# A three-block model on one core: how ten norms get their sums of squares, and how their tiles reach the products

## The reference

```python
def rms_norm(x, g):
    y = x * rsqrt(mean(x * x, axis=-1) + 1e-6)
    return y * g
# first block
h = x + stick_breaking_attention(rms_norm(x, norm_mix))
h = h + swiglu(rms_norm(h, norm_ffn))
h = h + sigmoid(rms_norm(h, norm_ple) @ w_gate) * (p @ w_proj)
x = rms_norm(h, final_norm)
# second block: gated convolution (31 taps) beside retention (4 heads)
u = rms_norm(x, norm_g) * (1 + scale) + shift
a = silu(layernorm(conv(a * sigmoid(b)))) @ conv_pw * silu(g)
h = x + gate * (concat(a, retention(u)) @ w_out)
x = rms_norm(h, final_g)
# third block: S5 beside SSD
h = x + concat(s5(rms_norm(x, norm_w)), ssd(...)) @ w_out
h = h + sigmoid(rms_norm(h, ple_norm_w) @ w_gate) * (p_3 @ w_proj)
return rms_norm(h, final_norm_w)
```

## Time and profile before

| what | value |
|---|---|
| median of 3 runs | 5034.85 us (5033.29 to 5037.63) |
| the profiled execution, its own time | 5034.92 us |
| its span | 5033.1 us |
| mean granted TensorE clock | 0.865 |
| TensorE matmuls, busy | 78% of the span |
| VectorE, busy | 51% |
| GpSimd, busy | 31% |
| ScalarE, busy | 17% |

### The profile page before, as it was taken

The page is one execution under the profiler, slowest core; times in us unless marked ns, Lnnn a source line. Parts: engine busy times, 40 slices in busy tenths (PEclk is TensorE's granted clock), DMA queues, the critical chain, the costliest instruction groups (busy, mean ns, idle before and its releaser), DMA issues.

```text
span 5033.1 us, 47576 instructions
## 1 busy us (share of the span) xinstructions
PE 3921.5 (78%) x18610; PEld 3141.9 (62%) x18610; DVE 2563.6 (51%) x2452; ACT 880.6 (17%) x1440; POOL 1549.5 (31%) x581
## 2 busy tenths in 40 slices
PE   4999996999999864777789886584996875559856
PEld 3667764878778753555556754463785764447745
DVE  5554565232332356777832342647149955444555
ACT  2433442000000022000010001202120111121021
POOL 2122213444444431555522321131323420004322
PEclk8999997989898887888899998797998976669978
DMA  1000000111111100111211111111631241112111
GB/s 65 25 26 26 22 22 30 51 51 55 49 50 50 58 29 17 59 58 58 75 46 42 56 44 58 34 58 67 121 78 55 87 131 25 25 42 75 59 34 50
DMA packets 140587, 259.59 MB, mean 52 GB/s; under 512 B 45744, under 2 KB 87728, under 8 KB 139184
## 3 DMA queue, kind: packets, MB, share of 16 engines
q1 hardware_dynamic: 50832, 156.26, 10.8%
q10 hardware_dynamic: 89632, 101.63, 6.3%
HBM read 209.35 MB, written 46.14 MB: 51 GB/s over the span
## 4 chain that ended last, share of the span: by engine, by line
PE 44%; issue 22%; DVE 18%; POOL 10%; ACT 2%; DMA 2%; ACTq 0%; POOLq 0%; DVEq 0%; SPq 0%
PE bank L474 12%; PE bank L475 11%; PE bank L476 11%; POOL wh L449 7%; POOL wl L451 3%; DVE acc L1429 2%; DVE sq L1445 1%; PE bank L685 1%; PE bank L648 1%; DVE rinv L1434 1%; DVE spill L1932 1%; DVE xl L1455 1%; PE bank L895 1%; DVE fb L1578 1%; PE bank L668 1%
## 5 line engine op out<-in xcount | busy, mean ns | idle before, releaser
L449 POOL TENSOR_TENSOR wh<-raw,mats 128x1024 fp32r<-128x1024 f32 x288 | 796.9, 2767 | 3399.4 <-PE bank L476 3347.8
L474 PE MATMUL bank<-xh,wh 128*128 128x512 f32 x3008 | 1206.8, 401 | 411.2 <-DVE xl L1455 155.9
L475 PE MATMUL bank<-xl,wh 128*128 128x512 f32 x3008 | 1194.3, 397 | 0.0
L476 PE MATMUL bank<-xh,wl 128*128 128x512 f32 x3008 | 1192.0, 396 | 0.0
L474 PEld LDWEIGHTS bank<-xh,wh 128*128 128x128 f32 x3008 | 580.9, 193 | 556.9 <-issue 295.7
L451 POOL TENSOR_TENSOR wl<-raw,wh 128x1024 fp32r<-128x1024 f32 x288 | 753.1, 2615 | 22.6
L476 PEld LDWEIGHTS bank<-xh,wl 128*128 128x128 f32 x3008 | 579.0, 192 | 124.5
L475 PEld LDWEIGHTS bank<-xl,wh 128*128 128x128 f32 x3008 | 581.3, 193 | 119.8
L1702 DVE SCALAR_TENSOR_TENSOR cacc<-apad,cols,cacc 128x1024 f32<-128x1024 f32 x232 | 346.4, 1571 | 0.0
L1578 DVE TENSOR_TENSOR_SCAN fb<-fb 128x256 f32<-128x256 f32 (+7 forms) x128 | 209.6, 1678 | 102.0 <-ACT ab L1027 102.0
L1475 DVE TENSOR_TENSOR h<-bank,h 128x512 f32<-128x512 f32 x240 | 164.9, 690 | 188.8 <-PE bank L476 188.8
(11 more groups left out here) (309 smaller groups left out, 5836.1 us busy)
## 6 DMA issues: line engine op xcount, KB each, us to landing
raw<-in_wstream SPq DMA_DIRECT2D x288, 512.0 KB, 3.6
spills<-spill ACTq DMA_DIRECT2D x40, 512.0 KB, 2.7
gate_spill<-gates ACTq DMA_DIRECT2D x16, 512.0 KB, 2.7
tabs<-in_rope ACTq DMA_DIRECT2D x4, 2048.0 KB, 8.2
f<-spills ACTq DMA_DIRECT2D x8, 1024.0 KB, 8.0
h<-in_x ACTq DMA_DIRECT2D x2, 2048.0 KB, 12.9
conv_spill<-cout ACTq DMA_DIRECT2D x8, 512.0 KB, 2.6
tabs<-gate_spill ACTq DMA_DIRECT2D x4, 1024.0 KB, 5.0
```

Source lines behind the costliest of these rows:

```text
L449: nc.gpsimd.tensor_tensor(wh[:, slot], raw[:, slot], ones, ALU.mult).then_inc(S("panel_high"), 1)
L474: nc.tensor.matmul(o, lh, rh, start=start, stop=False)
L475: nc.tensor.matmul(o, lh, rl, start=False, stop=False)
L476: return nc.tensor.matmul(o, ll, rh, start=False, stop=stop)
```

## The change

- Each tile is squared as soon as it is final. TensorE sums it by itself: eight f32 matmuls per tile with 128 tokens of squares as weights and one column of ones as the moving operand, accumulated over the tiles in bank 4. The sums lie with tokens on the partitions, [128, 8] for all 1024 tokens.
- These sums are put between the products that still run: before tiles 3 to 7 of an out product, behind units 7, 9, 11, 13 and 15 of `half7`, between the two units of panels 2 to 7 in a gate stage; the rest stand behind it.
- Root and reciprocal are taken on [128, 8]. `norm_spread` brings them back with eight matmuls against the identity, into banks 2 and 3 (and 5 and 6 for a second norm).
- Two norms in a row become one pass: squares are summed with and without the first gain, a second root is worked out from both, and the split for the next product is made before the kept norm (`norm_keep`).
- The split goes by halves of the tokens, 16 pieces with four buffers `hn`; the first product waits for each piece in turn (`split=`).
- In a side stage `pf` is loaded and split during an earlier stage; the side product starts ahead of the norm, whose spread comes before its tile 2, and ScalarE's high halves are interleaved with its copies.
- x is loaded by four DMAs, each waited for alone. `h_spill` is issued behind the spills of `s5_u`. The final output is stored tile by tile as it is scaled.
- Some loops lose their first or last turn to written-out code; some buffers are placed elsewhere.

The core of the diff:

```diff
+NORMS = [("mix", 1), ("ffn", 1), ("ple", 1), ("first_final", 2), ("conv_ln", 1), ("second_final", 2), ("ple3", 1),
+         ("last_final", 1)]
...
-            return dict(sq=sq, hn=sq, acc=sb("acc", [P, T], F32, stack), rinv=sb("rinv", [P, T], F32, stack))
+            return dict(sq=sb("sq", [P, 2, T], F32, stack), hn=sb("hn", [P, 4, HALF], F32, stack))
...
+                        if split is not None:
+                            pe.wait_ge(S("norm_low"), SPLIT0[split] + th * KT + n + 1)
                         t = slice(th * HALF, (th + 1) * HALF)
...
-            def norm_sums(n):
...
+            def norm_sum(name, k):
+                for j in range(SQUARES_OF[name]):
+                    n = SQUARES_OF[name] * k + j
+                    pe.wait_ge(S("norm_square"), SQUARES0[name] + n + 1)
+                    for c in range(CHUNKS):
+                        mm = nc.tensor.matmul(banks[4][:, KT * j + c:KT * j + c + 1], nb["sq"][:, n % 2, c * P:(c + 1) * P],
+                                              M["ones"][:, 0:1], start=k == 0 and c == 0 and j == 0, stop=k == KT - 1, skip_group_check=True)
+                    mm.then_inc(S("norm_summed"), 1)
+            def norm_spread(name, row, bank, sem):
+                pe.wait_ge(S("norm_inv"), INV0[name] + 1)
+                for c in range(CHUNKS):
+                    mm = nc.tensor.matmul(banks[bank + c // 4][:, c % 4 * P:(c % 4 + 1) * P],
+                                          rv[:, row, c:c + 1].broadcast_to([P, P]), M["ident"], start=True, stop=True)
+                    if c % 4 == 3:
+                        mm.then_inc(S(sem), 1)
+            def norm_end(name):
+                if SQUARES_OF[name] == 2:
+                    norm_spread(name, 5, 2, "norm_spread")
+                    norm_spread(name, 1, 5, "keep_spread")
+                else:
+                    norm_spread(name, 1, 2, "norm_spread")
+            def out_two(unit, panel, high, low, norm=None):
                 for n in range(KT):
+                    if norm is not None and n >= 3:
+                        norm_sum(norm, n - 3)
                     if n % 4 == 0:
...
                 attn_project(key)
+                if key[2] % 2 and key[2] >= 7:
+                    norm_sum("ffn", (key[2] - 7) // 2)
...
+            def side_product(name, n, norm):
...
                     if m % 4 == 0:
                         split_done(panels(name) + m // 4)
+                    if m == 2:
+                        norm_end(norm)
...
+            def gate(name, split, norm):
+                for p in range(KT):
+                    tile_x(units(name) + 2 * p, panels(name) + p, split=split if p == 0 else None,
+                           between=(lambda: norm_sum(norm, p - 2)) if p >= 2 else None)
+                for k in range(KT - 2, KT):
+                    norm_sum(norm, k)
+                norm_end(norm)
...
+            def norm_square(name, k, src=h, gain=None):
+                for j in range(SQUARES_OF[name]):
+                    n = SQUARES_OF[name] * k + j
+                    if n >= 2:
+                        act.wait_ge(S("norm_summed"), SQUARES0[name] + n - 1)
+                    if j == 0:
+                        i = A(nb["sq"][:, n % 2, :], src[:, k, :], ACT.Square)
+                    else:
+                        i = A(nb["sq"][:, n % 2, :], src[:, k, :], ACT.Square, scale=gain(k))
+                    i.then_inc(S("norm_square"), 1)
+            def norm_root(name):
+                A(rv[:, 4, 0:1], eps[:, 0:1], ACT.Sqrt)
+                act.wait_ge(S("norm_summed"), SQUARES0[name] + KT * SQUARES_OF[name])
+                A(rv[:, 0, :], banks[4][:, 0:CHUNKS], ACT.Sqrt, bias=eps[:, 0:1], scale=1.0 / D
+                  ).then_inc(S("norm_root"), 1)
+                if SQUARES_OF[name] == 2:
+                    act.wait_ge(S("norm_second"), sum(n == 2 and ROOT0[m] <= ROOT0[name] for m, n in NORMS))
+                    A(rv[:, 3, :], rv[:, 2, :], ACT.Sqrt, bias=eps[:, 0:1], scale=1.0 / D
...
+            def norm_high(name, i, mode="split"):
...
+                    act.wait_ge(S("norm_silu"), i + 1)
+                if mode == "mod":
+                    mm = A(xh[:, k, t], x, ACT.Identity, bias=mod[:, k:k + 1])
+                else:
+                    mm = A(xh[:, k, t], x, ACT.Copy)
+                mm.then_inc(S("norm_high"), 1)
...
-            act.wait_ge(S("setup"), 64)
-            norm(0, 0)
+            for k in range(KT):
+                act.wait_ge(S(f"x_in{k // 2}"), 16)
+                norm_square("mix", k)
+            norm_root("mix")
...
+            def side_take(name, norm):
                 for m in range(2 * KT):
                     th = m % 2
                     produced(act, units(name) + m)
                     A(side[:, m // 2, th * HALF:(th + 1) * HALF], banks[th][:, :], ACT.Copy
                       ).then_inc(S(f"bank_free{th}"), 1)
...
+            def gate_take(name, g, norm, gain):
                 for m in range(2 * KT):
                     produced(act, units(name) + m)
                     if m >= 2:
                         act.wait_ge(S("h_added"), 16 * g + m - 1)
                     A(sg[:, m % 2, :], banks[m % 2][:, :], ACT.Sigmoid).then_inc(S(f"bank_free{m % 2}"), 1)
+                    if m % 2 and m >= 3:
+                        norm_square(norm, m // 2 - 1, gain=gain)
+                act.wait_ge(S("h_added"), 16 * g + 16)
+                norm_square(norm, KT - 1, gain=gain)
+                norm_root(norm)
...
             if "s5_u" in run:
-                act.wait_ge(S("norm_scaled"), 7 * KT)
+                norm_highs("second_final")
+                spill_tiles("s5_u", 0, ACT.Copy, True)
...
                 act.dma_start(out[:, k, :], h[:, k, :]).then_inc(S("stored"), 16)
...
+            def norm_inverse(name):
+                n = ROOT0[name]
+                dve.wait_ge(S("norm_root"), n + 1)
+                if SQUARES_OF[name] == 1:
+                    V.reciprocal(rv[:, 1, :], rv[:, 0, :]).then_inc(S("norm_inv"), 1)
+                    return
+                link = Chain("norm_chain", 3 * sum(c == 2 and ROOT0[m] < n for m, c in NORMS))
+                link(V.reciprocal(rv[:, 1, :], rv[:, 0, :]))
+                link(V.tensor_tensor(rv[:, 2, :], rv[:, 1, :], rv[:, 1, :], ALU.mult))
+                V.tensor_tensor(rv[:, 2, :], rv[:, 2, :], banks[4][:, KT:KT + CHUNKS], ALU.mult
+                                ).then_inc(S("norm_second"), 1)
+                dve.wait_ge(S("norm_root"), n + 2)
+                link(V.reciprocal(rv[:, 4, :], rv[:, 3, :]))
+                V.tensor_tensor(rv[:, 5, :], rv[:, 4, :], rv[:, 1, :], ALU.mult).then_inc(S("norm_inv"), 1)
+            def norm_split(name, gain, mode="split", src=h):
+                hn, n0 = nb["hn"], SPLIT0[name]
+                spread = 2 * INV0[name]
+                def scale(i):
+                    th, k = i // KT, i % KT
                     if k == 0:
-                        V.tensor_copy(acc[:, :], nb["sq"][:, 0, :]).then_inc(S("norm_acc"), 1)
+                        dve.wait_ge(S("norm_spread"), spread + th + 1)
+                    if i >= 4:
+                        dve.wait_ge(S("norm_low"), n0 + i - 3)
+                    V.scalar_tensor_tensor(hn[:, i % 4, :], src[:, k, th * HALF:(th + 1) * HALF], gain(k),
+                                           banks[2 + th][:, :], ALU.mult, ALU.mult).then_inc(S("norm_scaled"), 1)
...
-                for th in range(2):
+                        mm = V.tensor_tensor(xl[:, k, t], hn[:, i % 4, :], xh[:, k, t].bitcast(F32), ALU.subtract)
+                    mm.then_inc(S("norm_low"), 1)
...
+            def norm_keep(gain, first):
...
-                if mode != "keep":
-                    low(KT - 1)
+                    if k == 0:
+                        dve.wait_ge(S("keep_spread"), first // KT + th + 1)
+                    V.scalar_tensor_tensor(h[:, k, t], h[:, k, t], gain(k), banks[5 + th][:, :], ALU.mult, ALU.mult
...
+                V.tensor_tensor(gg[:, :], modg[:, :], col("final_norm", 0, 8), ALU.mult).then_inc(S("gg_ready"), 1)
+                dve.wait_ge(S("gg_ready"), 2)
+                norm_inverse("first_final")
+                norm_split("first_final", lambda k: gg[:, k:k + 1], "mod")
...
+                for k in range(KT):
+                    for th in range(2):
+                        t = slice(th * HALF, (th + 1) * HALF)
+                        V.scalar_tensor_tensor(h[:, k, t], h[:, k, t], col("final_norm_w_3", k), banks[2 + th][:, :],
+                                               ALU.mult, ALU.mult).then_inc(S("h_final"), 1)
```

More of the change, by code:

```diff
@@ L484, in split_done, with tile @@
                 pe.wait_ge(S("panel_split"), panel.value(1))
-            def tile(unit, slot, slabs, rhs, between=None):
+            def tile(unit, slot, slabs, rhs, between=None, split=None):
                 for th in range(2):
@@ L496, in tile, with tile_x @@
```

(49 more changed lines are left out.)

327 lines of the change are left out of this document (156 added, 171 removed).

## The result

The changed kernel took 4921.9 us (median of 4 runs, 4917.95 to 4923.52) where the kernel before took 5036.2 (5033.29 to 5040.56): a ratio of 0.9769, 95% interval 0.9757 to 0.9782. The forecast was 4890 in a range of 4835 to 4950, and faster: the sign and the range held, and of the 144.4 us of gain 114.4 came.

A forecast was written before the change was run, and what follows sets the result against it. TensorE was taken as the bound, busy 3921.5 of 5033.1 us and waiting on sums of squares and low halves around norms. Gains of 11.2 + 12.2 + 67.8 + 28.5 - 2.3 + 18.0 + 9.0 = 144.4 gave 4890 us, range 4835 to 4950.

The forecast's parts named there:

- The price of a sum: Each tile's sum on TensorE was taken as 16 records, 1.8 us between warm products and 3.5 us cold.
- The layer norm: From last centring to two units done: 58.2 us with eight cold sums, against 55.9 before, a loss of 2.3.
- the side stages: Both stages with their norms: 56.9 us each against 90.7, loading and splitting pf earlier; gain 67.8 us together.
- The split by halves: At each norm TensorE follows the split tile by tile: 23.5 us from first scaling, against 32.5 before.
- two units done: End point of each norm's length: two units of 24 products each, a unit taking 5.45 us warm.
- rival (c): Sums behind the stream run warm: first and layer norm gain 14 each, others 22 together; 4840 us, chance 0.17.
- Rival (b): Bursts of sums cool TensorE inside the stream: 2 us restart at each of 32 places, 64 more; 4955, chance 0.15.
- 10 sums 17.8: Ahead of the third block, ten sums between products of the out product lengthen TensorE's stream by 17.8 us.
- The third block: Two norms ahead of it take 64.4 us against 87.4; after a charge of 5 for the save, gain 18.0.
- The h save: The 4 MB save meets the gather of u, z's spills queue behind it: charged 5 us, bounds 0 and 15.
- The first norm: x in four parts, eight cold sums, first scaling at 43.3, done at 66.8 us against 78.0: gain 11.2.
- a norm is over when two units are done: Each norm was counted as over for TensorE with two units done, before the change 12.9 us after the first product.

The follow-up runs named there:

- the rounded squares: Changed kernel with squares and ones column rounded to fp32r and two moving columns, 8 records per sum instead of 16: 4806.5 us, ratio 0.9536.
- the spread sums: Changed kernel, but ahead of the third block one sum stands after each 6 products instead of two after 12: 4909.0 us, ratio 0.9739.
- the sixteen sums in a row: Changed kernel, but all sixteen sums of the two norms ahead of the third block stand behind the stream: 4923.2 us, ratio 0.9773.
- the last kernel: Changed kernel plus early h save, fp32r squares, early gates' load, sums apart, and only the third block's angles ahead of first-norm roots: 4788.2 us, ratio 0.9511.

## Why the prediction was right, and where its sizes were off

**Right, by the steps as they were put.** The price of a sum, 1.8 warm and 3.5 cold, measured 1.84 and 3.43; the record is the unit, as the rounded squares show by halving it. The range held, but it was 115 us wide, and the size is off by 30 us: places that gave 36.0 and 0.7 us too little stand against 9.2 that others gave too much, and that these offset each other is luck. The waits on squares and low halves went. The two full-width reciprocals of 6.57 us became 0.59 us of idle time. The layer norm's first scaling comes 31.5 us after the last centring (3083.84 to 3115.30), 32.2 forecast. The first block's two norms in a row have their first scaling 18.1 us behind the gate's last product (1880.42 to 1898.54), 18.3 forecast. The load and split of pf, 9.9 us, were part of the side stages' gain, as the run with the load put back shows. The forecast for the last norm was 9.0, and 8.3 came.

**The split by halves, and the 9.2 us too much.** From the first scaling to two units done the prediction had 23.5 us, against 32.5 with a single wait. Measured are 21.6 at the first norm, the FFN and the third block, 22.7 at the convolution and 24.8 at the layer norm (26 forecast); with the single wait put back, 33.6 at the FFN. So following tile by tile is worth 12, not 9.0, and 1.9 us of that were gained on the forecast. At the FFN two units were done after 38.5 us (44.1 forecast): besides the split, eight sums took 14.3 us where 17.8 were charged, as a sum between attention's last units takes the place of short waits there, and those behind the stream ran partly warm. Some 3 of these 5.6 us were lost again inside the FFN, where no run shows why. The 7.0 us at the side stages are not the split's: from the side product's start to the gate's second unit it took 39.7 and 38.3 us, 39.1 forecast. They are rival (c), true in small: the three sums right behind warm products, at a clock of 0.91 in the first, put off the side product by 5.5 us in both stages, where 8.9 were charged.

**Rival (c) fell where it had most to give.** The layer norm's 128 records ran back to back for 27.4 us and stayed at 0.50, and the first norm's eight took the same 3.43 us each. The Trainium skill ("TensorE: Matmul & The Clock Gate", the HAM clock gate) lets a busy TensorE rise to its full clock. The layer norm's row does not agree: TensorE is busy throughout it with one-column matmuls, the clock stays at 0.50, and the measurement decides.

**Rival (b) is true for pairs of sums and false for single ones.** It was priced as one restart of 2 us at each of 32 places. Single sums never cooled anything: the places ahead of the FFN and of the side norms, and the third block's gate, show 1.84 us and warm products throughout. Pairs did: 1.6 us at three of the six places in the first block's gate, as much as the convolution's shortfall of 4.6; and 2.5 us at each of five places ahead of the third block. Together that is 17.5 us where (b) had 64. The step that failed is "10 sums 17.8": they cost 30.5 in that stream.

**The third block** has 15.0 us of the shortfall. The pairs are 12.7 of it, and the spread sums won back 11.5. The h save was charged 5 and cost 11.4, inside its bounds of 0 and 15, and by another way than the one named: it held up SyncE's gathers and with them the weights, not z's spills. The save's own 11.1 us in the earlier trace rows would have been the better charge. Work that the sum had too dear makes up for the rest: the last six sums at 17.4 where 19.0 were charged, and the split's 1.9.

**The first norm** has 10.3 us. Its own terms held: T0, the first scaling, at 42.7 (43.3 forecast), two units done at 64.3 (66.8). The step that failed is that a norm is over when two units are done. What stood behind the old wait was costed at nothing without being listed: ScalarE's table loads and a wait on VectorE ahead of qT, 8.9 us, and 2.2 of cold restart behind it; 2 more went in the attention, and no run shows where. The layer norm's 6.1 us are the same mistake: its two units were done 56.3 us after the centring (58.2 forecast), and then came 5.1 us of wait for a load that ScalarE issues only behind the whole split, and 2.2 of restart. Both costs were at nothing because they had been covered, and each time the cover was the idle time that the change removed.

## What to carry to other kernels

When a long wait is shortened, list everything that every engine and queue does during it and just behind it: what lay under the wait comes out, here 8.9 us at the first norm and 5.1 at the layer norm, and cheap reordering puts it back under cover. Let the consumer wait for what it reads, half tile by half tile, before anything else is tried; that wait was 64 of 114 us. Matmuls of one or two columns cost by the record, so choose the type and shape with fewest records before choosing their place, if the rounding can be borne. Where they stand between products, put them singly: two of these bursts in a row cooled the products behind them, at all five places in the last out product and at three of six in a gate, and the same two apart did not.

## What the runs showed of the hardware

- A matmul with the squares as weights and one or two moving columns costs by its records: 0.115 us each at full clock and 0.21 at half, the same for f32 with one column (two records) and fp32r with two (one record). Wider moving operands are no part of this comparison.
- Matmuls of one or two columns, back to back for 27.4 us (f32) and 13.8 (fp32r) in the layer norm, stayed at a granted clock of 0.50, and the sixteen sums in a row, which start behind warm products, at 0.54 in the mean.
- In the first norm the granted clock reads 1.00 while the same 16 records take 3.43 us, as at 0.50 elsewhere. At the start of these runs the records' own pace tells the clock, and the clock's row does not.
- While a 4 MB save and the gathers of u were under way together, SyncE's issue of two gathers lasted 11.8 us, and 1.2 without the save.
- Some VectorE operations on 32 elements took 2.2 us instead of 0.19 while GpSimd split a panel. VectorE's and GpSimd's timelines of the last kernel:

```profile
62.64 0.19 DVE L1636 TENSOR_TENSOR s5c<-s5p 128x32 f32<-128x32 f32 x1
62.87 2.22 DVE L1637 TENSOR_TENSOR s5c<-s5p 128x32 f32<-128x32 f32 x1
65.12 0.19 DVE L1638 TENSOR_TENSOR s5p<-s5c 128x32 f32<-128x32 f32 x1
65.34 2.22 DVE L1639 TENSOR_TENSOR s5c<-s5p 128x32 f32<-128x32 f32 x1
```

```profile
62.69 2.34 POOL L463 TENSOR_TENSOR wh<-raw,mats 128x1024 fp32r<-128x1024 f32 x1 [7.36 <-PE bank L490]
65.11 2.40 POOL L465 TENSOR_TENSOR wl<-raw,wh 128x1024 fp32r<-128x1024 f32 x1
```

  One such operation ends with each of GpSimd's, as if it waited for that to end, however short it is itself. The earlier trace rows had shown this on tiles of 512 elements alone.
